# Stream 0's transposes ahead of a modulation piece, small loads in two lots, and four row pieces of layer 2's modulation moved into the dense feed-forward

## What is computed

```
mod = silu(cvec) @ ada_w[l] + ada_b[l]
sh1, sc1, g1, sh2, sc2, g2 = split(mod, 6)
o, new = token_mixer(rms_norm(x, norm1_g[l]) * (1 + sc1) + sh1, ...)
x = x + g1 * o
x = x + g2 * channel(rms_norm(x, norm2_g[l]) * (1 + sc2) + sh2, l)
```

## Time and profile before

| | us |
|---|---|
| three runs | 1637.39, 1633.57, 1634.72 (median 1634.72) |
| profiled execution, its time | 1634.51 |
| its span | 1632.9 |
| TensorE busy | 1533.8 (94%) |
| VectorE busy | 1173.0 (72%) |
| ScalarE busy | 914.4 (56%) |
| GpSimd busy | 66.5 (4%) |

### The profile page before, as it was taken

How to read it: one execution, slowest core, us unless ns; L and a number is a source line. 1 busy time by engine, 2 the same in 40 slices (tenths; PEclk the granted TensorE clock), 3 DMA queues, 4 the chain that set the end, 5 groups by cost and what they waited for, 6 DMA issues and landing times.

```text
span 1632.9 us, 19705 instructions
## 1 busy us (share of the span) xinstructions
PE 1533.8 (94%) x7058; PEld 1179.3 (72%) x7058; DVE 1173.0 (72%) x1215; ACT 914.4 (56%) x789; POOL 66.5 (4%) x105
## 2 busy tenths in 40 slices
PE   6888879999998777999999999999999999999997
PEld 3555447888656544888888888888888888888885
DVE  1364564445436354688889888888889888889988
ACT  1213234344231313577877877877877777777774
POOL 1500000000001000100000000000000000000200
PEclk9998999999998698899999999999999999999999
DMA  9969978865686266699999999999999999999992
GB/s 355 325 204 413 338 239 268 266 204 199 235 284 190 106 233 232 235 397 369 378 380 367 391 388 370 383 375 376 392 363 385 387 363 386 379 377 370 396 403 117
DMA packets 192569, 523.26 MB, mean 320 GB/s; under 512 B 10624, under 2 KB 71200, under 8 KB 187400
## 3 DMA queue, kind: packets, MB, share of 16 engines
q1 hardware_dynamic: 167440, 493.39, 82.0%
q0 software_dynamic: 6768, 18.63, 3.3%
q10 hardware_dynamic: 18312, 10.60, 2.1%
HBM read 505.49 MB, written 17.08 MB: 320 GB/s over the span
## 4 chain that ended last, share of the span: by engine, by line
PE 82%; DVE 8%; ACT 4%; DMA 3%; issue 2%; SPq 0%; ACTq 0%; DVEq 0%
PE PS L601 21%; PE PS L603 21%; PE PS L602 21%; PE PS L716 5%; PE PS L607 5%; DMA ring<-in_ada_w 2%; PE PS L931 2%; PE PS L682 2%; DVE parts L2033 1%; PE PS L746 1%; PE PS L730 1%; ACT parts L1431 1%; PE PS L621 1%; ACT arena L1274 1%; DMA ring<-in_w_in 1%
## 5 line engine op out<-in xcount | busy, mean ns | idle before, releaser
L2033 DVE TENSOR_TENSOR parts<-ring,parts 128x2048 fp32r<-128x2048 f32 x336 | 766.3, 2291 | 109.2 <-ACT parts L1431 107.0
L1431 ACT ACTIVATE parts<-ring 128x2048 fp32r<-128x2048 f32 x336 | 643.9, 1919 | 216.6 <-PE PS L603 216.5
L601 PE MATMUL PS<-parts 128*128 128x512 f32 x1608 | 633.5, 394 | 8.1 <-DVE parts L1678 4.1
L603 PE MATMUL PS<-parts 128*128 128x512 f32 x1608 | 627.8, 390 | 0.0
L602 PE MATMUL PS<-parts 128*128 128x512 f32 x1608 | 627.5, 390 | 0.0
L601 PEld LDWEIGHTS PS<-parts 128*128 128x128 f32 x1608 | 302.6, 188 | 74.0 <-DVE parts L2033 7.1
L603 PEld LDWEIGHTS PS<-parts 128*128 128x128 f32 x1608 | 302.4, 188 | 64.2
L602 PEld LDWEIGHTS PS<-parts 128*128 128x128 f32 x1608 | 302.7, 188 | 61.9 <-issue 0.2
L1592 DVE TENSOR_TENSOR parts<-ring,parts 128x2048 fp32r<-128x2048 f32 x33 | 75.5, 2289 | 52.8 <-PE PS L603 50.0
L716 PE MATMUL PS<-ring,xnT 128*128 128x420 f32 (+1 forms) x240 | 91.7, 532 | 0.0
L1215 ACT ACTIVATE parts<-ring 128x2048 fp32r<-128x2048 f32 x33 | 63.0, 1916 | 29.6 <-PE PS L603 29.6
(11 more groups left out here) (310 smaller groups left out, 932.0 us busy)
## 6 DMA issues: line engine op xcount, KB each, us to landing
ring<-in_moe_w SPq DMA_DIRECT2D x336, 1024.0 KB, 6.9
ring<-in_ada_w SPq DMA_DIRECT2D x40, 1024.0 KB, 8.5
ring<-in_w_in SPq DMA_DIRECT2D x32, 840.0 KB, 11.6
ring<-in_ffn_w SPq DMA_DIRECT2D x44, 512.0 KB, 5.0
ring<-in_w_out SPq DMA_DIRECT2D x16, 1024.0 KB, 7.8
ring<-in_ffn_w SPq DMA_DIRECT2D x11, 1024.0 KB, 4.8
expert_rows<-zeros ACTq DMA_DIRECT2D x17, 512.0 KB, 4.2
ring<-in_ada_w SPq DMA_DIRECT2D x16, 512.0 KB, 11.3
```

What stands on the lines that cost most here:

```text
L601: mm(out, s_hi, m_hi, start=start, stop=False)
L603: return mm(out, s_lo, m_hi, start=False, stop=stop)
L1431: A(w_hi(j), slot(n), ACT.Copy).then_inc(hi_ready, 1)
L2033: TT(w_lo(j, 3), slot(W0 + j), w_hi(j).bitcast(f32), ALU.subtract).then_inc(split_done, 1)
```

## The change

- TensorE: stream 0's eight transposes stand ahead of the fourth piece of `first_rows(0)`; `first_columns(0)` follows the rows at once, and stream 1's eight transposes come behind it.
- GpSimd: the ten gains of a layer count on a semaphore of their own (`gain_in`). In layer 1 the other thirteen small loads are issued once two units of the input projection have been copied. The norms and gates wait for the gains only; the mixer waits for the other lot.
- Layer 1's schedule has five tokens `a` less. Group 3 has four row pieces left in it. Its other four loads stand in the list between stream 1's `w_out` loads and the first up weight. TensorE runs two of the row pieces behind stream 0's up pieces, two behind stream 1's transposes, and the column piece behind stream 1's up pieces. VectorE and ScalarE walk their parts of the five pieces at the start of `dense_ffn`; ScalarE's split of the third up weight stands there too.
- Two waits follow the columns: the second feed-forward block on TensorE waits for them, for it uses PSUM bank 2, and stream 1's output projection waits for one column piece less.

```diff
--- before.py
+++ after.py
@@ -42,7 +42,7 @@
 A0 i1 A0 i1 A0 i1 A0 B0 i1 B0 i1 n1 B0 i1 B0 B0 t0 i1 C0 t0 t0 i1 C0 i1 C0 i1 A1 A1 C0 g1 C0 l1 c1 A1 C0 A1 C0
 """}
 PHASE_2 = {0: """
-A1 l1 a A1 a c1 a a A1 a A1 B1 a B1 a B1 a o0 o0 B1 B1 a C1 t1 a C1 t1 t1 a C1 o0 a o0 a a C1 a C1 a a o0 C1 r0 r0 a C1
+A1 l1 a A1 a c1 a a A1 a A1 B1 a B1 B1 a o0 o0 B1 B1 a C1 t1 C1 t1 t1 a C1 o0 a o0 a C1 C1 a a o0 C1 r0 r0 C1
 """, 1: """
 a B1 a B1 a B1 o0 o0 B1 B1 a C1 t1 C1 t1 t1 a C1 o0 a o0 C1 a C1 a o0 C1 r0 r0 a C1
 """}
@@ -348,8 +348,10 @@
                     up_kv_load(l, 1)
                 if token == "A1" and i == 0:
                     g_after_1.append(g_ada)
+            if l == 0:
+                g_ada += 1
             early_of.append(g_ada)
-            assert at_piece["i1"] == 9 and at_piece["o0"] == 4 and at_piece["a"] % 9 == 8
+            assert at_piece["i1"] == 9 and at_piece["o0"] == 4 and at_piece["a"] % 9 == (8 if l else 3)
             assert [at_piece[x] for x in ("A0", "A1", "B0", "B1", "C0", "C1")] == [3, 3, 4, 4, 6, 6]
             assert [at_piece[x] for x in ("t0", "t1", "n1", "g1", "l1", "c1")] == [2, 2, 0, 0, 0, 0] and at_piece["r0"] == 1
             for i in range(4):
@@ -359,6 +361,9 @@
                     first["w2", f] = add(2048, rows(I["ffn_w2"][0], 2 * f, 2 * f + 2, 0, D), a=2)
 
                 for f in range(N_FF):
+                    if f == 0:
+                        for k in range(4, 8):
+                            ada_load(EARLY + 2, k)
                     first["up", f, 0] = add_up(f, 0)
                     first["up", f, 1] = add_up(f, 1)
                     if f:
@@ -412,6 +417,7 @@
         split_done = sem("split_done")
         first_in, x_in = sem("first_in"), sem("x_in")
         small_in = [sem(f"small_in{l}") for l in range(DEPTH)]
+        gain_in = [sem(f"gain_in{l}") for l in range(DEPTH)]
         adab_in = [sem(f"adab_in{i}") for i in range(2)]
         out_sem = [sem("out_sem0"), sem("out_sem1")]
         state_out = [sem("state_out0"), sem("state_out1")]
@@ -486,7 +492,7 @@
 
 
         N_FIRST = 5
-        N_SMALL = len(GAIN) + 4 + 2 * 2 * 2 + 1
+        N_SMALL = 4 + 2 * 2 * 2 + 1
 
         @block.gpsimd
         def _(pool):
@@ -496,15 +502,17 @@
                 else:
                     pool.wait_ge(Q["h_ready"], 5)
 
-                def load(dst, src, **how):
-                    pool.dma_start(dst, src, **how).then_inc(small_in[l], 16)
+                def load(dst, src, s=small_in[l], **how):
+                    pool.dma_start(dst, src, **how).then_inc(s, 16)
 
                 for name in GAIN:
                     if name == "m0":
                         src = I["state_mlstm_m"][0:1, l, :, :].rearrange("a d h -> a (d h)")
                     else:
                         src = I[name][l:l + 1, :]
-                    load(G(l, name), src.broadcast_to([128, src.shape[1]]))
+                    load(G(l, name), src.broadcast_to([128, src.shape[1]]), gain_in[l])
+                if l == 0:
+                    pool.wait_ge(Q["h_ready"], 2)
                 load(ctx_k[:, l, :], I["cache_swa_k"][0, l].rearrange("t g d -> t (g d)"))
                 load(ctx_v[:, l, :], I["cache_swa_v"][0, l].rearrange("t g d -> t (g d)"))
                 load(ctx_ckv[:, l, :], I["cache_mla_ckv"][0, l])
@@ -647,6 +655,8 @@
                 if half:
                     wait("out_h", 1)
                 for i in range(4 * half, 4 * half + 4):
+                    if i == 3:
+                        norm_T(0, 0, 0)
                     w = weights(first["ada", 0, i])
                     for kk in range(2):
                         k = 2 * (i % 4) + kk
@@ -666,9 +676,8 @@
 
             def modulation():
                 first_rows(0)
-                norm_T(0, 0, 0)
+                first_columns(0)
                 norm_T(0, 0, 1)
-                first_columns(0)
 
             def first_in_proj():
 
@@ -921,7 +930,7 @@
                 wait("oT_a", 2 * l + s + 1)
                 wait("oT_d", 2 * l + s + 1)
                 if s == 1:
-                    wait("turned_out", early_of[l])
+                    wait("turned_out", early_of[l] - (l == 0))
                 t = oT(s)
                 for i in range(4):
                     n, half = i // 2, i % 2
@@ -947,6 +956,8 @@
 
                 def up(f, half, s):
                     hi, lo = split_weights(first["up", f, half])
+                    if f == 1 and half == 0 and s == 0:
+                        wait("turned_out", EARLY + 3)
                     if half == 0 and f >= 2:
                         wait("hT_ready", 2 * (f - 2) + s + 1)
                     for k in range(4):
@@ -983,10 +994,15 @@
                 wait("xs_ready", 1)
                 up(0, 0, 0)
                 up(0, 1, 0)
+                next(ada)
+                next(ada)
                 norm_T(0, 1, 1)
+                next(ada)
+                next(ada)
                 wait("xs_ready", 2)
                 up(0, 0, 1)
                 up(0, 1, 1)
+                next(ada)
                 for f in range(1, N_FF):
                     up(f, 0, 0)
                     up(f, 0, 1)
@@ -1387,11 +1403,13 @@
 
             def dense_start():
 
-                for n in (first["up", 0, 1], first["up", 1, 0]):
-                    split_hi(n)
+                split_hi(first["up", 0, 1])
 
             def dense_ffn():
                 act.wait_ge(zeros_ready, 4)
+                split_hi(first["up", 1, 0])
+                for i in range(5):
+                    next(ada)
                 for f in range(N_FF):
                     for b in range(3 * f, min(3 * f + 3, 2 * N_EXP + 1)):
                         act.dma_start(XY[b].rearrange("p (a c) -> p a c", a=8),
@@ -1513,8 +1531,9 @@
                 if l == 1:
                     for i in range(KD + 1):
                         next(ada)
+                act.wait_ge(gain_in[l], 16 * len(GAIN))
+                gates_B(l, 0)
                 act.wait_ge(small_in[l], 16 * (N_SMALL + l))
-                gates_B(l, 0)
                 mixer(l, ada)
                 next(out1)
                 norm(l, 1, 0)
@@ -2149,11 +2170,12 @@
                 if l == 1:
                     for i in range(KD + 1):
                         next(ada)
-                dve.wait_ge(small_in[l], 16 * (N_SMALL + l))
+                dve.wait_ge(gain_in[l], 16 * len(GAIN))
                 norms_A(l, 0)
                 gates_B(l, 0)
                 norms_C(l, 0)
                 log_gates_B(l, 0)
+                dve.wait_ge(small_in[l], 16 * (N_SMALL + l))
                 mixer(l, ada)
                 dve.wait_ge(state_out[l], 16 * 3)
                 out1 = out_proj(l, 1)
```

## The result

The changed kernel takes 1651.13 us (median of four runs, 1647.18 to 1654.15) against 1635.53 us of the kernel before beside it (four runs, 1633.57 to 1637.39): ratio 1.0094, interval 1.0069 to 1.0119, so 15.6 us slower. Built again later, beside other runs of the kernel before, it was 13.5 us slower (ratio 1.0076, interval 1.0060 to 1.0093). The prediction had the sign and 7.8 us of it; the time is past the upper end of the range.

A forecast was written before the change was run, and what follows sets the result against it. TensorE, carrying 82% of the chain, was taken as the bound. Hand-over 8.4 us lost, less 0.3 for layer 1's mixer and 0.3 for the start, gave 7.8 us slower: 1634.5 to 1642.3 us, range 1636.0 to 1647.5.

The forecast's parts named there:

- Parts 1 and 2: Start of the kernel: earlier transposes and small loads in two lots gain 1.5 us, cost 1.2: 0.3 us gained.
- The price of the second lot: Start: ScalarE's copy ahead of group A's scores waits for the second lot's landing, 1.2 us lost.
- read to the full for 4.4 us: Start: each small load taken out of the stretch speeds up w_in, giving the upper bound of 4.4 us.
- Part 3: Layer 1's mixer: of five pieces taken out only one row piece is on the chain, 0.3 us gained.
- Part 4: Hand-over to feed-forward: moved ada_w loads delay the first up weight; stream 1's input ready at 251.7 instead of 245.71.
- themselves cost nothing: Hand-over: the four row pieces and eight transposes lie in TensorE's wait for stream 1's norm, costing 0 us.
- Part 5: Ahead of the second feed-forward block: columns, copies and split in a row leave TensorE idle 3.5 us; up pieces take 6.6.
- The clock behind the hole: Second feed-forward block: a lower clock after the 3.5 us hole costs up to 2.0 us more, left to the range.
- The dearest hand-over and the late lot: Rival: small lot lands 3.5 us late and hand-over costs 12: 15 us slower, 1649.7 us; chance 0.03.
- The hidden load: Rival: up weights land before stream 0's transposes, only the columns' cost is paid: 0.9 us slower, 1635.4; chance 0.12.
- the faster case: Rival: TensorE's own work sets layer 1's pace, so removed pieces come off whole: 6.5 us faster, 1628.0; chance 0.07.

The follow-up runs named there:

- e13: The kernel before, unchanged, profiled a second time: 1635.87 us in one profiled execution.
- e2: Kernel before plus only the move of five modulation pieces and their loads from layer 1's mixer into the feed-forward: 1649.25 us against 1635.68, ratio 1.0077.
- e4: Changed kernel with two modulation pieces left in layer 1's mixer moved from behind group C's scores to the gaps around the transposes ahead: 1645.12 us against 1635.68.
- e3: Changed kernel with the four ada_w loads behind the first two up weights in the list of loads: 1642.25 us against 1635.68, ratio 1.0046.
- e11: Kernel before with only stream 0's transposes put ahead of the fourth modulation piece: 1635.02 us against 1635.08, ratio 0.9994.
- e12: The changed kernel, built and profiled a second time: 1648.59 us against 1635.08 for the kernel before, ratio 1.0076.
- e5: Changed kernel with ScalarE's split of the first up weight behind stream 0's normed columns: 1643.35 us against 1635.97, ratio 1.0050.
- e7: e3 with VectorE's split of the third up weight ahead of its copies of the column piece: 1638.81 us against 1635.97, ratio 1.0009.

## Why the prediction was right in sign and wrong in size

**Parts 1 and 2: right in mechanism, the number by luck.** Forecast 0.3 us gained, with the wait for `w_in` ending near 48.3 and the scores released by the copy that waited for the second lot. Measured 48.56, that release, and 68.42 - 68.16 = 0.26. That this is so near is luck: group A's scores start at 67.45 to 68.46 in the seven profiles with both parts and the wait for the second lot, and at 68.40 to 69.93 in the three with neither part (before, e13, e2). The price of the second lot was taken at 1.2 us; the copy of the transposes starts 67.50 - 55.14 = 12.4 us after the end of the second copy of the projection, against 11.4 before and 12.6 forecast, so the price was 1.0. GpSimd's queue falls from 30.6% of the DMA engines' time in 47 to 50 us to 0.7%, but the wait ends only 1.25 us earlier: the Trainium skill's rule that all queues share the engines (DMA: Bandwidth & Descriptors, Issuing engines are not separate DMA queues), read to the full for 4.4 us, did not decide the time.

**Part 3: the step that failed.** "The others stand where TensorE then waits for VectorE or ScalarE", so costing and saving nothing. That they did not hold up the chain was so; that they could be taken away for nothing was not. They were TensorE's only work in those gaps, and without them the clock fell for the scores behind: 3.3 us lost for 0.3 gained, and 5.8 lost in the five profiles where the projection's first pair was slow as well. e4 shows it: one line of the schedule puts the pieces back at those gaps, and the scores are back. The prediction weighed the clock only at the place where pieces were added, and not where they were taken away.

**Part 4: right in mechanism, short in size.** ScalarE's first split started 12.5 us after the output projection (235.60 - 223.10) where before it started 0.7 after it (217.82 - 217.15), the columns right behind it. The load was ready 5.4 us after TensorE's second group (230.21 to 235.60), forecast 4.9. Then stream 1's input: forecast 251.7 - 217.15 = 34.6 us after the projection's start, measured 258.84 - 223.10 = 35.7. The other 0.7 is from the term that the four pieces "themselves cost nothing": stream 0's up pieces began at half pace (0.43 us a matmul, twelve of them), so that the first two row pieces ran until 253.7 where the norm of stream 1 was done at 252.7, and stream 1's transposes stood behind them. In e3, where the up pieces began earlier, TensorE waited 0.57 us there and the pieces cost nothing.

**Part 5: the hole right, the clock short.** Hole forecast 3.5 us, measured 269.44 - 266.2 = 3.2, and in the order forecast. Stream 1's two up pieces were taken at 6.6 us and took 266.2 - 258.84 = 7.4: the first nine matmuls again at 0.43. The Trainium skill's rule on the clock (TensorE: Matmul & The Clock Gate, Part 1: The HAM clock gate) would have had them at full pace behind the pieces in the wait; here 2.2 us of waiting stood between, and the row disagrees with what was drawn from it, 1.0 us less. The clock behind the hole, "up to 2.0 us more", was left to the range; it was 1.6 us, in all six profiles with the hole, and belonged into the sum.

**The sum with what was measured**: hand-over 10.3 (9.3 against the 37.0 us of e13), clock in the mixer 3.3, clock behind the hole 1.6, start -0.3. One thing more: from the feed-forward's end to layer 2's router seven profiles of kernels with parts 3 to 5 took 209.3 to 209.9 us (the first of the changed kernel, with 212.4, apart) and six without them 210.6 to 211.1: some 1.3 us less, of a cause that stays open. Together 12.6 to 13.6 us, and 2.5 more where the projection's first pair is slow too, against medians of 13.5 and 15.6. The profiled execution of the changed kernel is 19.7 us of span longer. Of the rest, 2.2 us are group A's scores of stream 1, 4.80 us here and in e4, e11 and e12, 2.60 in the other ten, e3, e5 and e7 with the same instructions up to there among them; some 3 are the 212.4, which e12, the same kernel, did not repeat (209.8); some 1 us stays open.

**The rivals.** The dearest hand-over and the late lot (15 us) gave nearly the time measured first, but by another way: the clock was low behind both waits, as that rival had it, but the lot was not late and layer 1's 3.3 us were not in it. The hidden load fell by ScalarE's 11.72 us, the faster case by layer 1's 3.3.

## What to carry to other kernels

Work that stands in a wait of the busiest engine is not free to take away: ask what the granted clock does there without it, and price the work behind at both levels. A load put into a ring ahead of others moves the slot, and so the release, of every load after it; follow the first one whose release becomes late to the engine whose queue stands behind its user. And where a small step is put ahead of a long one on an engine in order, turn the two if nothing needs the small one first: here the loss went from 6.6 us (e3) to 2.8 (e7).

## What the runs showed of the chip that was not expected

Two waits of 4.06 and 1.40 us, with 3.3 to 3.6 us of transposes between them, went with a second fall of the clock and scores of 4.5 us behind; with a piece of 1 us in the second, and 3.2 to 3.3 us of idle time in the first, the same 24 matmuls took 2.9. That held in all 14 profiles; the two waits were not varied one at a time. Elsewhere the same instructions ran at either level from one execution to the next: group A's scores of stream 1 (2.60 or 4.80 us), and, in the changed kernel's two profiles, the first pair of the output projection (7.1 or 9.7). That is some of the spread of several us between executions of one kernel, and a reason to read the same stretch in several profiles before a few us are put down to an edit.
